# Bias tiles turned by PE transposes, the memory source in the bias buffer's free part, and output projections begun inside the attentions' last steps

## The chip, the cores and the metric

The kernel runs on one NeuronCore of a Trainium2 chip. The metric is the device time of one execution in microseconds. TensorE is called PE here, VectorE DVE, ScalarE ACT, GpSimd POOL and SyncE SP, as in the profile.

## The reference, cut to what matters

Three transformer blocks follow each other on one sequence of 256 tokens with 1024 features, all in float32. The first has a gated linear attention and "moba", a causal attention with a bias by relative position; the second a stick-breaking attention, a memory attention and 32 routed experts; the third two layers, l0 and l1, each a feed-forward (ffn1), a mixer, a memory attention and a feed-forward again. The change lies in moba and in the mixers and memory attentions of the two layers. What these compute:

```python
# moba (8 heads), dsa (8 heads, over selected keys), band (16 heads); masked keys get -inf
logits = einsum('bqhd,bshd->bhqs', q, k) * dh ** -0.5 + bias_table[bucket(qpos - kpos)]
o = einsum('bhqs,bshd->bqhd', softmax(logits), v)
# diff (4 heads, two maps each, one bias per head)
attn = p[:, :, 0] - lam * p[:, :, 1]
out_b = rmsnorm(einsum('bhqs,bshe->bqhe', attn, v), subln_g) * (1.0 - lambda_init)
# l0: h + concat([dsa, diff]) @ w_out; l1: h + band @ w_out
# memory attention of each layer, m = rmsnorm(mem, src_gain)
k, v = split(m @ wkv, 2); k = rmsnorm(k); q = rmsnorm(h @ wq)
o = softmax(q @ k.T * M_DIM ** -0.5) @ v;  h = h + o @ wo
```

## The kernel before

Activations lie feature-major in SBUF as tiles of 128 features x 256 tokens: `tile(X, i)`, T = 256, P = 128, eight tiles for 1024 features. Weights come as a stream of 2 MB chunks through five slots `W`; SP's queue loads a chunk when the semaphore `released` says that the one five before it is done with, and PE raises `released` in order, on the first matmul behind a chunk's last use (`end_chunk`, `pending`). Every engine's program is one straight list, so the order of work is the order of the code; engines wait for each other by semaphores. PSUM has eight banks of 128 x 512: banks 0 to 3 are a ring that `ring_bank` deals out in turn, 4 to 7 are given by name (`banks.begin`). A bank that is begun again is waited for until the engine that reads it has emptied it.

All of PE's matmuls but a few go through the helper `mm` and so show as L600. One float32 matmul leaves two records in the trace. `turn_probs` (L890) transposes with one record each.

A biased attention runs in `softmax_pairs`: step p issues the scores of heads 2p and 2p+1 into two ring banks, then whatever `fill(p)` holds, then the values of pair p-3 (bank 7), then the transposes of the probabilities of pair p-2 (banks 5 and 6). DVE takes the maxima and scales the exponentials, ACT makes the exponentials (L1728) and copies turned probabilities and outputs out of PSUM (L1647). The exponentials of a head wait until the probabilities of four heads before are turned, and ACT copies turned probabilities after a step's exponentials.

The bias of a head is added by PE: a table in DRAM is read with overlapping rows into `A`, 512 columns a head, so that a matmul with the anti-identity `REV` as stationary operand puts the reversed bias into the bank, and the scores are accumulated on top. `load_bias` fetches this on POOL's queue.

In the layers the memory keys and values (`layer_memory_half`, eight halves of eight or four matmuls each) are the fill of diff and of band; their source is loaded into `H` when the projections are done with it, and ACT multiplies it by its gains (`memory_gains`). Behind the attention stands `down(f"{l}_w_out", ...)`, the output projection, in banks 4 to 7 with the sums of the memory keys' norm between its parts, and then `memory`: two query units, the scores of four heads, transposes, results, projection. `gates` of the first block are the fill of moba.

The norms outside `BY_LOG` take a square root on ACT and a reciprocal on DVE; those in it take a logarithm and an exponential on ACT.

## Time and profile before

| | us |
|---|---|
| median of 3 runs | 3049.65 (3047.19 to 3058.12) |
| profiled execution | 3052.73 |
| its span | 3050.9 |
| PE busy | 2906.7 |
| DVE busy | 1356.4 |
| ACT busy | 600.1 |
| first bias to gates 7's end, moba | 157.2 to 231.4 |
| diff and dsa with the output projection, l0 | 2034.0 to 2137.2 |
| band with the output projection, l1 | 2689.7 to 2790.7 |

A busy PE is one with a matmul in flight; matmuls overlap, so a row's duration is longer than the distance to the next start. A row of the timeline merges instructions of one kind; in brackets stands how long the engine was idle before it and what released it.

### The profile page before, as it was taken

How to read it: one execution, taken by the hardware profiler on the slowest of the kernel's cores; microseconds unless marked ns; L12 is line 12 of the kernel's file. 1: busy time of each engine (PE TensorE's matmuls, PEld its weight loads, DVE VectorE, ACT ScalarE, POOL GpSimd, SP SyncE). 2: the span in 40 equal slices, each digit the busy share in tenths (PEclk: the TensorE clock that was granted, in tenths of full speed). 3: DMA queues.
4: the chain of work that ended last, by engine and by line, in shares of the span. 5: the costliest groups of instructions: out<-in, count | busy, mean ns of one | idle time of the engine just before them, and what ended most of it. 6: DMA issues, size and time to landing. Idle time of an engine off the chain costs nothing.

```text
span 3050.9 us, 44763 instructions
## 1 busy us (share of the span) xinstructions
PE 2906.7 (95%) x18718; PEld 2251.9 (74%) x18718; DVE 1356.4 (44%) x2555; ACT 600.1 (20%) x1249; POOL 13.0 (0%) x22
## 2 busy tenths in 40 slices
PE   8999999999999898999899899999999999989999
PEld 7988999868543333343343699986899999967999
DVE  5432896422211111112111576655566665643665
ACT  2220331221211111111011210233210110242210
POOL 0000000000000000000000000000000000000000
PEclk9999999999899999999999999999999999999999
DMA  6333544334899999999999644541344444523341
GB/s 247 139 111 140 192 166 169 136 110 166 352 432 431 432 432 430 433 431 433 429 431 432 277 174 173 193 165 60 111 170 169 187 166 174 213 97 111 139 166 70
DMA packets 39026, 723.83 MB, mean 237 GB/s; under 512 B 4220, under 2 KB 4348, under 8 KB 7504
## 3 DMA queue, kind: packets, MB, share of 16 engines
q1 hardware_dynamic: 35280, 705.73, 57.7%
q0 software_dynamic: 3584, 15.74, 1.5%
q8 instruction: 127, 2.08, 0.3%
q14 instruction: 35, 0.29, 0.0%
HBM read 720.32 MB, written 1.12 MB: 236 GB/s over the span
## 4 chain that ended last, share of the span: by engine, by line
PE 83%; DMA 12%; DVE 2%; ACT 2%; issue 1%; SPq 0%; POOL 0%; ACTq 0%; DVEq 0%
PE ps L600 64%; DMA sb_weights<-stream 12%; PE ps L1462 9%; PE ps L1482 4%; PE ps L1440 2%; PE ps L1400 2%; PE ps L890 1%; DVE sb_x L2436 0%; ACT sb_weights L1647 0%; PE ps L1428 0%; DVE sb_h L2187 0%; ACT sb_weights L1728 0%; DVE sb_squares L2155 0%; PE ps L1495 0%; ACT sb_k L2041 0%
## 5 line engine op out<-in xcount | busy, mean ns | idle before, releaser
L600 PE MATMUL ps<-sb_h,sb_weights 128*128 128x128 f32 (+1 forms) x3488 | 565.1, 317 | 23.5 <-DMA sb_weights<-stream 7.9
L600 PEld LDWEIGHTS ps<-sb_h,sb_weights 128*128 128x128 f32 x3488 | 503.8, 193 | 66.4 <-issue 12.9
L1462 PE MATMUL ps<-sb_weights,sb_k 128*64 128x512 f32 x1536 | 340.2, 595 | 16.5 <-DMA sb_weights<-stream 9.8
L2834 DVE TENSOR_TENSOR sb_v<-ps,sb_small 128x256 f32<-128x256 f32 x128 | 48.4, 420 | 667.1 <-PE ps L1428 667.1
L600 PE MATMUL ps<-sb_weights 128*128 128x256 f32 (+1 forms) x1744 | 302.9, 331 | 8.0 <-ACT sb_weights L1647 6.5
L600 PEld LDWEIGHTS ps<-sb_weights 128*128 128x128 f32 x1744 | 269.2, 192 | 35.4 <-ACT sb_weights L1647 7.1
L1462 PEld LDWEIGHTS ps<-sb_weights,sb_k 128*64 128x64 f32 x1536 | 109.6, 137 | 216.5 <-issue 204.1
L600 PE MATMUL ps<-sb_v,sb_weights 128*128 128x128 f32 x2240 | 265.4, 276 | 0.0
L600 PEld LDWEIGHTS ps<-sb_v,sb_weights 128*128 128x128 f32 x2240 | 257.6, 192 | 0.0
L600 PE MATMUL ps<-sb_a,sb_weights 128*128 128x128 f32 (+1 forms) x1512 | 205.5, 293 | 1.1 <-DVE sb_a L2614 1.1
L1482 PE MATMUL ps<-sb_weights,sb_k 128*64 128x512 f32 x768 | 173.5, 605 | 31.2 <-DMA sb_weights<-stream 30.7
L600 PEld LDWEIGHTS ps<-sb_a,sb_weights 128*128 128x128 f32 x1512 | 192.9, 192 | 8.2 <-issue 1.5
L1482 PEld LDWEIGHTS ps<-sb_weights,sb_k 128*64 128x64 f32 x768 | 55.5, 139 | 133.6 <-issue 133.6
L600 PE MATMUL ps<-sb_r,sb_weights 128*128 128x128 f32 x1256 | 149.8, 276 | 0.0
L600 PEld LDWEIGHTS ps<-sb_r,sb_weights 128*128 128x128 f32 x1256 | 144.9, 192 | 0.0
L2041 ACT ACTIVATE sb_q<-ps 128x512 f32<-128x512 f32 x64 | 38.2, 597 | 461.2 <-PE ps L1462 461.2
L1462 PE MATMUL ps<-sb_a,sb_k 128*64 128x512 f32 x512 | 113.4, 595 | 7.9 <-ACT sb_k L2041 7.9
L1792 ACT ACTIVATE sb_v<-ps 128x256 f32<-128x256 f32 x120 | 46.0, 384 | 341.1 <-PE ps L600 334.3
L1647 ACT ACTIVATE sb_v<-ps 128x256 f32<-128x256 f32 (+1 forms) x59 | 24.6, 416 | 367.6 <-PE ps L600 367.6
L2480 DVE TENSOR_TENSOR sb_weights<-ps,sb_v 128x256 f32<-128x256 f32 x160 | 63.2, 420 | 74.2 <-PE ps L600 73.9
L2331 DVE TENSOR_TENSOR sb_weights<-sb_weights 128x1024 f32<-128x1024 f32 (+1 forms) x80 | 94.8, 1186 | 0.0
L1462 PEld LDWEIGHTS ps<-sb_a,sb_k 128*64 128x64 f32 x512 | 38.8, 137 | 71.3 <-issue 71.3
(358 smaller groups left out, 3403.1 us busy)
## 6 DMA issues: line engine op xcount, KB each, us to landing
sb_weights<-stream SPq DMA_DIRECT2D x72, 4096.0 KB, 28.1
sb_weights<-stream SPq DMA_DIRECT2D x142, 2048.0 KB, 7.8
sb_a<-stream SPq DMA_DIRECT2D x24, 4096.0 KB, 27.7
sb_a<-tables POOLq DMA_DIRECT2D x2, 2048.0 KB, 16.6
sb_a<-tables POOLq DMA_DIRECT2D x2, 1536.0 KB, 14.1
sb_weights<-stream SPq DMA_DIRECT2D x2, 1024.0 KB, 7.6
sb_a<-tables POOLq DMA_DIRECT2D x2, 1024.0 KB, 7.8
sb_h<-mem POOLq DMA_DIRECT2D x2, 1024.0 KB, 5.1
```

Source lines behind the costliest of these rows:

```text
L600: ins = pe.matmul(out, lhsT, rhs, start=start, stop=stop, skip_group_check=skip)
L890: ins = pe.transpose(PS[b][:, n * P:(n + 1) * P], probs[:, t * T + s * P:t * T + (s + 1) * P], ident)
L1400: ins = pe.matmul(PS[4 + m // 2][:, (m % 2) * T:(m % 2 + 1) * T], Y_TOK[:, m * P:(m + 1) * P], SPREAD, start=False, stop=last, skip_group_ ...
L1440: ins = pe.matmul(ps[:, q * PAIR:(q + 1) * PAIR], H_TOK[:, t * D + d * P:t * D + (d + 1) * P], PICK[:, t * PAIR:(t + 1) * PAIR], start=t = ...
L1462: ins = pe.matmul(ps[own[e], :], XG[:, k * PAIR + e * LOT:k * PAIR + (e + 1) * LOT], w[e](k * 512, 512), start=k == 0, stop=k == KT - 1)
L1482: ins = pe.matmul(ps[n][own[e], :], HID[:, k * PAIR + e * LOT:k * PAIR + (e + 1) * LOT], w[e]((k % 4) * D + n * 512, 512), start=k == 0, s ...
L1647: act.activation(dst, src(b), func, scale=scale).then_inc(banks.emptied[b], 1)
L1792: act.activation(KEPT[i], PS[b][:, 0:T], ACT.Copy).then_inc(sem("kept"), 1)
L2041: act.activation(dst, PS[fill[0]][:, 0:cols], ACT.Copy).then_inc(L.emptied[fill[0]], 1)
L2331: dve.tensor_tensor(part(0, 1), part(1, 1), part(0, 1), ALU.subtract).then_inc(done, 1)
L2480: return dve.tensor_tensor(by_tile(dst)[:, :, t * P:(t + 1) * P], by_tile(PS[b][:, 0:T]), by_tile(kept), ALU.add)
L2834: ins = dve.tensor_tensor(by_lot(z, s), by_lot(PS[TURNED[c][0]][:, :], s), bias.unsqueeze(3).broadcast_to([P, 2, 2, LOT]), ALU.add)
```

## The change

The bias of a head is now 256 columns of `A` and one transfer, with the table stored the other way round. Three 128 x 128 transposes, each with a block of the table as stationary operand and `REV` as moving one, put it into the bank (`biases`); the scores are accumulated on top as before. The masked corner is one memset. The half of `A` that this frees takes the memory source (`MEM`), which POOL fetches right behind the bias, and ACT scales in two parts during the projections.

Fills move. In band, halves 0 to 6 of the memory units fill steps 0 to 6 (before: 0 to 7 in steps 2 to 9), with units in banks 7 and 4 in place of the ring; in diff, seven halves remain. Half 7 goes into the memory attention, between scores 2 and 3, with its weight chunk kept back (`keep_back`, `end_kept`) and scores 3 in bank 5. moba's gates go to bank 4. The output projections (`layer_out`) use banks 0 to 3; their first 40 matmuls stand in the attentions' last three steps, before values and transposes; the sums of the memory keys and the rest come after. For l0 the diff tiles come first, and w_out's two chunks are swapped in the stream. The sums of `l0_nsub` go behind dsa's first pair. Three norms join `BY_LOG`. Band starts when the first two key tiles are normalized (`band_ready`).

```diff
+            def biases(b, head):
+                for s, t in ((0, 0), (0, 1), (1, 1)):
+                    at = head * T + (t - s) * P
+                    pe.matmul(PS[b][:, t * T + s * P:t * T + (s + 1) * P], A[:, at:at + P], REV[:, :],
+                              start=s == t == 0, stop=False, is_transpose=True, skip_group_check=True)
...
-            def softmax_pairs(name, fill=lambda p: None):
+            def softmax_pairs(name, fill=lambda p: None, ready=lambda p: None):
...
                         for e in range(2):
-                            for t in range(2):
-                                cols = keys(True, t)
-                                mm(PS[bs[e]][:, cols], REV[:, :], A[:, (2 * p + e) * 512:(2 * p + e + 1) * 512][:, cols],
-                                   t == 0, False, True)
-                                if a.get("mask") is not None:
-                                    mm(PS[bs[e]][:, cols], ident, a["mask"][:, cols], False, False, True)
+                            biases(bs[e], 2 * p + e)
+                            for t in range(2 if a.get("mask") is not None else 0):
+                                mm(PS[bs[e]][:, keys(True, t)], ident, a["mask"][:, keys(True, t)], False, False, True)
...
+        OUT_IN_TAIL = [(range(4), range(4)), (range(4), range(4, KT)), ((4,),)]
...
+            def layer_out(l, js, ms=range(KT)):
+                name, src = f"{l}_w_out", tiles(O, 8) if l == "l1" else tiles(O, 4, 4) + tiles(O, 4)
+                if js[0] == 0:
+                    for i in range(ms[0] // 2, ms[-1] // 2 + 1):
+                        banks.begin(pe, (name, i), i)
+                if js[0] in (0, 4) and ms[0] == 0:
+                    out_weights[0] = next_chunk()
+                w, last = out_weights[0], js[-1] == KT - 1
+                order = [(j, 2 * i + m) for i in range(4) for j in js for m in range(2)] if last else [
+                    (j, m) for j in js for m in ms]
+                for j, m in order:
+                    if m == ms[0] and l == "l0":
+                        if j >= 4:
+                            banks.wait_emptied(pe, ("dsa", "out", j - 4))
+                        elif j % 2 == 0:
+                            norm_part(pe, "l0_nsub", j // 2)
+                    elif m == ms[0]:
+                        banks.wait_emptied(pe, ("band", "out", j))
+                    ins = mm(PS[m // 2][:, (m % 2) * T:(m % 2 + 1) * T], w[:, (j % 4) * D + m * P:(j % 4) * D + (m + 1) * P],
+                             src[j], j == 0 and m % 2 == 0, j == KT - 1, True)
...
                     logits(2)
-                    logits(3)
+                    layer_memory_half(l, 7)
+                    logits(3, bank=5)
...
-            softmax_pairs("moba", lambda p: fm_unit("gates", h, p))
-            fm_unit("gates", h, 7)
+            softmax_pairs("moba", lambda p: fm_unit("gates", h, p, bank=4))
+            fm_unit("gates", h, 7, bank=4)
...
+                        for n in {0: (0, 1), 1: (2,), 5: ()}.get(i, (i + 2,)):
+                            layer_memory_half(l, n, bank=4 if n == 6 else None)
...
-                    sums("l0_nsub")
                     pe.wait_ge(sem("dsa_mask"), 2)
-                    softmax_pairs("dsa")
-                    banks.wait_emptied(pe, ("dsa", "out", 3))
+                    def dsa_fill(p):
+                        if p == 0:
+                            sums("l0_nsub", (5, 6))
+                        if p >= 4:
+                            layer_out(l, *OUT_IN_TAIL[p - 4])
+                    softmax_pairs("dsa", dsa_fill)
...
-                    softmax_pairs("band", lambda p: layer_memory_half(l, p - 2) if 2 <= p <= 9 else None)
-                    banks.wait_emptied(pe, ("band", "out", 7))
-                down(f"{l}_w_out", tiles(O, 8), {1: lambda: pe.wait_ge(sem("subln_scaled"), 1)} if l == "l0" else {},
-                     between={1: lambda: sums(f"{l}_nmk")})
+                    def band_ready(p):
+                        if p % 2 == 0 and p < 8:
+                            norm_part(pe, "l1_nk", p // 2)
+                        if p == 3:
+                            for c in range(2):
+                                banks.wait_emptied(pe, ("l1_v", "common", c))
+                    def band_fill(p):
+                        if p < 7:
+                            layer_memory_half(l, p, bank=7 if p < 2 else 4)
+                        elif p > 7:
+                            layer_out(l, *OUT_IN_TAIL[p - 8])
+                    softmax_pairs("band", band_fill, band_ready)
+                sums(f"{l}_nmk", (5, 6))
+                layer_out(l, (5,))
+                layer_out(l, (6, 7))
...
-                    squares("l0_nsub", lambda eng, part: [banks.wait_emptied(eng, ("diff", "out", 2 * part + q)) for q in range(2)])
-                    softmax_pairs("dsa")
+                    squares_only("l0_nsub", lambda eng, part: [banks.wait_emptied(eng, ("diff", "out", 2 * part + q)) for q in range(2)])
+                    softmax_pairs("dsa", lambda p: roots("l0_nsub") if p == 0 else
+                                  squares_only("l0_nmk", x_ready("l0_mem_k")) if p == 4 else None)
...
-                for key in [("iq", 0), ("iq", 1)] if l == "l0" else [("l1_v", "common", 1)]:
-                    banks.wait_filled(pool, key)
-                pool.dma_start(H[:, :], mem3_d).then_inc(sem(f"{l}_mem_loaded"), 16)
+                pool.dma_start(MEM[l], mem3_d).then_inc(sem(f"{l}_mem_loaded"), 16)
```

In PE's list, band begins as follows before the change: the projection's last rows, then bias (moving `sb_a`, stationary `sb_reversal`) and scores (`sb_k,sb_q`) of pair 0, and the bias of pair 1 at once.

```order
1019 L600 MATMUL ps<-sb_weights,sb_r 128x256 x8
1020 L600 MATMUL ps<-sb_a,sb_reversal 128x128
1021 L600 MATMUL ps<-sb_a,sb_reversal 128x256
1022 L600 MATMUL ps<-sb_a,sb_reversal 128x128
1023 L600 MATMUL ps<-sb_a,sb_reversal 128x256
1024 L600 MATMUL ps<-sb_k,sb_q 128x128 x2
1025 L600 MATMUL ps<-sb_k,sb_q 128x256 x2
1026 L600 MATMUL ps<-sb_a,sb_reversal 128x128
```

The same place after the change, where `sb_a,sb_weights` is half of a memory unit:

```order
990 L603 MATMUL ps<-sb_weights,sb_r 128x256 x8
991 L885 MATMUL ps<-sb_reversal,sb_a 128x128 x6
992 L603 MATMUL ps<-sb_k,sb_q 128x128 x2
993 L603 MATMUL ps<-sb_k,sb_q 128x256 x2
994 L603 MATMUL ps<-sb_a,sb_weights 128x256 x8
995 L885 MATMUL ps<-sb_reversal,sb_a 128x128 x6
```

Four bias matmuls of a pair became six transposes, and a memory half moved between the first pairs.

In PE's list, dsa ends as follows before the change: values (`sb_weights,sb_v`), transposes of probabilities (`sb_const,...`, L890), and behind the last values the output projection (`sb_weights 128x256`) with the sums of the memory keys.

```order
770 L890 MATMUL ps<-sb_const,sb_squares 128x128 x6
771 L600 MATMUL ps<-sb_weights,sb_v 64x256 x2
772 L600 MATMUL ps<-sb_weights,sb_v 64x128 x2
773 L890 MATMUL ps<-sb_const,sb_weights 128x128 x6
774 L600 MATMUL ps<-sb_weights,sb_v 64x256 x2
775 L600 MATMUL ps<-sb_weights,sb_v 64x128 x2
776 L890 MATMUL ps<-sb_const,sb_squares 128x128 x6
777 L600 MATMUL ps<-sb_weights,sb_v 64x256 x2
778 L600 MATMUL ps<-sb_weights,sb_v 64x128 x2
779 L600 MATMUL ps<-sb_weights 128x256 x16
780 L600 MATMUL ps<-sb_squares,sb_const 128x256 x4
```

The same place after the change (L934 is `turn_probs` there):

```order
737 L934 MATMUL ps<-sb_const,sb_squares 128x128 x6
738 L603 MATMUL ps<-sb_weights 128x256 x16
739 L603 MATMUL ps<-sb_weights,sb_v 64x256 x2
740 L603 MATMUL ps<-sb_weights,sb_v 64x128 x2
741 L934 MATMUL ps<-sb_const,sb_weights 128x128 x6
742 L603 MATMUL ps<-sb_weights 128x256 x16
743 L603 MATMUL ps<-sb_weights,sb_v 64x256 x2
744 L603 MATMUL ps<-sb_weights,sb_v 64x128 x2
745 L934 MATMUL ps<-sb_const,sb_squares 128x128 x6
746 L603 MATMUL ps<-sb_weights 128x256 x8
747 L603 MATMUL ps<-sb_weights,sb_v 64x256 x2
748 L603 MATMUL ps<-sb_weights,sb_v 64x128 x2
```

Between the last three groups of values and transposes, 16, 16 and 8 matmuls of the projection now stand.

On ACT, the start of dsa before the change has the roots of `l0_nsub` (Sqrt, `sb_squares<-ps`) ahead of the first exponentials (`sb_softmax_stats` rows), with a table load on either side.

```order
414 L1699 ACTIVATE sb_squares<-ps,sb_const 128x512 x2
415 L1728 ACT_TABLE_LOAD
416 L1728 ACTIVATE sb_weights,sb_softmax_stats<-ps,sb_softmax_stats 128x128
417 L1728 ACTIVATE sb_weights,sb_softmax_stats<-ps,sb_softmax_stats 128x256
418 L1728 ACTIVATE sb_weights,sb_softmax_stats<-ps,sb_softmax_stats 128x128
```

After the change:

```order
415 L1788 ACTIVATE sb_weights,sb_softmax_stats<-ps,sb_softmax_stats 128x256
416 L1745 ACT_TABLE_LOAD
417 L1762 ACTIVATE sb_squares<-ps,sb_const 128x512
418 L1763 ACTIVATE sb_squares<-sb_squares 128x512
419 L1762 ACTIVATE sb_squares<-ps,sb_const 128x512
420 L1763 ACTIVATE sb_squares<-sb_squares 128x512
421 L1788 ACTIVATE sb_squares,sb_softmax_stats<-ps,sb_softmax_stats 128x128
```

The roots, now logarithms and exponentials, stand between the exponentials of pair 0 and those of pair 1.

## Rows read from the trace of the kernel before

**Rows 1.** The page, part 1: busy time, share of the span, instructions.

```profile
PE 2906.7 (95%) x18718; PEld 2251.9 (74%) x18718; DVE 1356.4 (44%) x2555; ACT 600.1 (20%) x1249; POOL 13.0 (0%) x22
```

**Rows 2.** The page, part 4: the chain that ended last.

```profile
PE 83%; DMA 12%; DVE 2%; ACT 2%; issue 1%; SPq 0%; POOL 0%; ACTq 0%; DVEq 0%
```

**Rows 3.** PE's timeline, steady part of band: start us, us, instructions merged.

```profile
2715.17 0.87 PE L600 MATMUL ps<-sb_weights,sb_v 128*64 128x256 f32 x8
2715.97 0.87 PE L890 MATMUL ps<-sb_const,sb_squares 128*128 128x128 f32 x6
2716.68 1.48 PE L600 MATMUL ps<-sb_a,sb_reversal 128*128 128x128 f32 x8
2718.09 0.93 PE L600 MATMUL ps<-sb_k,sb_q 64*128 64x128 f32 x8
2718.95 3.72 PE L600 MATMUL ps<-sb_h,sb_weights 128*128 128x256 f32 x16
2722.60 0.87 PE L600 MATMUL ps<-sb_weights,sb_v 128*64 128x256 f32 x8
```

**Rows 4.** Line L890 in band: count, duration ns min/median/max, first and last start.

```profile
L890 PE MATMUL ps<-sb_const,sb_weights x24: 272/273/330, 2707.5 to 2753.4; 128*128 128x128 f32 x24
```

**Rows 5.** PE's timeline from the last projection before band to the query.

```profile
2686.22 3.62 PE L600 MATMUL ps<-sb_weights,sb_r 128*128 128x256 f32 x16
2693.49 2.90 PE L600 MATMUL ps<-sb_a,sb_reversal 128*128 128x128 f32 x8 [3.65 <-issue]
...
2761.24 7.14 PE L600 MATMUL ps<-sb_weights 128*128 128x256 f32 x32 [0.68 <-ACT sb_weights L1647]
...
2790.67 7.07 PE L600 MATMUL ps<-sb_h,sb_weights 128*128 128x256 f32 x32
```

**Rows 6.** Waits of PE, 2689 to 2791: us in total, times, longest.

```profile
PE ps L600 <- ACT sb_weights L1728: 2.9, 4, 0.8
PE ps L600 <- ACT sb_weights L1647: 1.6, 2, 1.0
```

**Rows 7.** PE's timeline, diff and dsa of l0 up to the query.

```profile
2034.02 1.58 PE L600 MATMUL ps<-sb_a,sb_reversal 128*128 128x128 f32 x8
...
2076.30 1.97 PE L600 MATMUL ps<-sb_squares,sb_const 128*128 128x256 f32 x8 [1.08 <-ACT sb_squares L1681]
2078.10 0.38 PE L600 MATMUL ps<-sb_a,sb_reversal 128*128 128x128 f32 x2
...
2081.67 0.49 PE L600 MATMUL ps<-sb_a,sb_reversal 128*128 128x128 f32 x2
...
2097.56 0.87 PE L600 MATMUL ps<-sb_weights,sb_v 128*64 128x256 f32 x8 [2.58 <-ACT sb_weights L1647]
...
2137.21 7.07 PE L600 MATMUL ps<-sb_h,sb_weights 128*128 128x256 f32 x32
```

**Rows 8.** Two stretches: length, PE, PEld, DVE, ACT, POOL busy, granted clock, DMA share.

```profile
2100.00:2108.00 8.00, 6.26 (x26) 4.13 (x27) 6.56 (x7) 3.71 (x8) 0.00 (x0) 0.50 0.01 2
2710.00:2750.00 40.00, 38.34 (x215) 25.63 (x214) 15.60 (x65) 13.20 (x54) 0.00 (x0) 1.00 0.15 53
```

**Rows 9.** DVE's timeline: the first maxima of dsa, behind the mask.

```profile
2081.77 0.62 DVE L2305 TENSOR_REDUCE sb_softmax_stats<-ps 128x1 f32<-128x128 f32 x2 [11.02 <-PE ps L600]
```

**Rows 10.** PE's timeline in moba: pairs 1 and 3.

```profile
168.35 1.55 PE L600 MATMUL ps<-sb_a,sb_reversal 128*128 128x128 f32 x8 [1.75 <-ACT sb_weights L1728]
...
188.61 1.55 PE L600 MATMUL ps<-sb_a,sb_reversal 128*128 128x128 f32 x8 [0.83 <-ACT sb_weights L1728]
```

**Rows 11.** DVE's timeline in moba: the copy of gate 0.

```profile
167.90 0.68 DVE L2253 TENSOR_TENSOR sb_a<-ps,sb_rstd 128x512 f32<-128x512 f32 x1
```

**Rows 12.** PE's timeline, memory attention of l0: scores 3, and the next query.

```profile
2158.39 2.08 PE L600 MATMUL ps<-sb_r,sb_q 128*128 128x256 f32 x4 [1.90 <-ACT sb_weights L1728]
...
2183.71 7.07 PE L600 MATMUL ps<-sb_h,sb_weights 128*128 128x256 f32 x32
```

**Rows 13.** DMA issues, 2000 to 2250: count, KB each, median us to landing.

```profile
sb_weights<-stream SPq DMA_DIRECT2D x14, 2048.0 KB, 7.8
```

More of the change, by code:

```diff
@@ L186, in stream_of @@
             out += [columns(w)]
-        out += [columns(g("mem_wkv")), rows(g("w_out")), columns(g("mem_wq")), rows(g("mem_wo"))]
+        w = rows(g("w_out"))
+        out += [columns(g("mem_wkv")), w[::-1] if l == "l0" else w, columns(g("mem_wq")), rows(g("mem_wo"))]
         out += [up_pairs(g("ffn2_wg"), g("ffn2_wu")), rows_22(g("ffn2_wd"))]
@@ L651, in fm, with fm_unit @@
                             between[2 * c + u]()
-            def fm_unit(name, src, u, norm=None):
+            def fm_unit(name, src, u, norm=None, bank=None):
                 w = next_chunk() if u % 2 == 0 else half_used[0]
                 half_used[0] = w
-                b = ring_bank((name, u))
+                b = ring_bank((name, u)) if bank is None else banks.begin(pe, (name, u), bank)
                 for m in range(2):
@@ L693, in layer_memory_half @@
                 if not second:
-                    half_used[0] = next_chunk() if u % 2 == 0 else half_used[0]
-                    ring_bank(key)
-                w, (b, _) = half_used[0], banks.of[key]
+                    memory_used[0] = next_chunk() if u % 2 == 0 else memory_used[0]
+                    ring_bank(key) if bank is None else banks.begin(pe, key, bank)
+                w, (b, _) = memory_used[0], banks.of[key]
                 for j in range(KT):
@@ L753, in down @@
                     end_chunk()
+            out_weights = [None]
+            def layer_out(l, js, ms=range(KT)):
[18 more added lines that the diff above has]
+                             src[j], j == 0 and m % 2 == 0, j == KT - 1, True)
+                    if last and j == KT - 1 and m % 2:
+                        ins.then_inc(banks.filled[m // 2], 1)
+                if js[-1] % 4 == 3 and ms[-1] == KT - 1:
+                    end_chunk()
             def begin_norm(name):
@@ L795, in first_sums, with sums @@
                 ins.then_inc(banks.filled[b], 1)
-            def sums(name):
+            def sums(name, at=None):
                 n = NORMS[name]
@@ L802, in sums @@
                 for u in range(-(-groups // 2)):
-                    b = ring_bank((name, u))
+                    b = ring_bank((name, u)) if at is None else banks.begin(pe, (name, u), at[u])
                     for g in range(2 * u, min(2 * u + 2, groups)):
@@ L818, in softmax @@
                         b = ring_bank((name, "logits", i))
-                        biased = a["bias"] is not None
-                        causal = "causal" in a
-                        for t in range(2 if biased else 0):
-                            cols = keys(causal, t)
-                            mm(PS[b][:, cols], REV[:, :], A[:, i * 512:(i + 1) * 512][:, cols], t == 0, False, True)
-                            if a.get("mask") is not None:
-                                mm(PS[b][:, cols], ident, a["mask"][:, cols], False, False, True)
                         for t in range(2):
                             qs, ks = a["q"](i, t), a["k"](i)
-                            cols = keys(causal, t)
+                            cols = keys("causal" in a, t)
                             for j in range(len(qs)):
-                                ins = mm(PS[b][:, cols], qs[j], ks[j][:, 0:cols.stop - cols.start], not biased and j == 0,
+                                ins = mm(PS[b][:, cols], qs[j], ks[j][:, 0:cols.stop - cols.start], j == 0,
                                          j == len(qs) - 1, True)
@@ L1074, in query, with logits @@
                     fm_unit(f"{name}_q", tiles(H, 8), u, qn if u == 0 else None)
-                def logits(h):
-                    b = ring_bank((name, "logits", h))
+                def logits(h, bank=None):
+                    b = ring_bank((name, "logits", h)) if bank is None else banks.begin(pe, (name, "logits", h), bank)
                     banks.wait_emptied(pe, (f"{name}_q", h // per_unit))
@@ L1887, in project_kept, with memory_gains @@
                 keep(3, fourth, banks.emptied[fourth])
-            def memory_gains(l):
+            def memory_gains(l, part):
                 act.wait_ge(sem(f"{l}_mem_loaded"), 16)
-                for i in range(KT):
-                    act.activation(tile(H, i), tile(H, i), ACT.Identity, scale=S(f"{l}_mem_src_norm", i, i + 1)
+                for i in range(4 * part, 4 * part + 4):
+                    act.activation(tile(MEM[l], i), tile(MEM[l], i), ACT.Identity, scale=S(f"{l}_mem_src_norm", i, i + 1)
                                    ).then_inc(sem(f"{l}_mem_scaled"), 1)
```

106 lines of the change are left out of this document (56 added, 50 removed).

## The prediction

> **What bounds the kernel now.** I read the page's busy times first: TensorE (PE) is busy 95% of the span, the vector engine (DVE) 44%, the scalar engine (ACT) 20% [rows 1]. The chain that ended last is 83% PE and 12% DMA, the latter the experts' weights, which the change leaves alone [rows 2]. So outside the experts a microsecond of PE work removed, or of PE waiting filled, comes off the span unless something else ends later. Touched are four attentions (moba; diff and dsa in layer l0; band in layer l1) and, in each layer, the output projection and the memory attention behind them. There I read PE's timeline in starts: the distance of two starts prices what lies between, without the overlap of pipelined ends. A stage's span less the sum of its parts is what it loses.
>
> **Term 1, the bias.** In the steady part of band a pair of heads takes 1.41 us for its bias (2716.68 to 2718.09, eight records for four matmuls), 0.86 for scores, 3.65 for half a memory unit, 0.80 for values, and 0.71 for six transposes of probabilities (2715.97 to 2716.68), so 0.118 each [rows 3]. The change does a pair's bias with six transposes of that 128x128 shape, each with a stationary operand of its own, as those have. Before: 20 pairs (moba 4, diff 4, dsa 4, band 8) x 1.41 = 28.2; after: 20 x 0.71 = 14.2. That is -14.0, all of it PE time, and it is contained in terms 2 to 4. The dsa masks stay ordinary matmuls. The records of such a transpose last 0.273 though they start 0.118 apart [rows 4]; I take the starts, since only they delay the next instruction.
> The Trainium skill ("TensorE: Matmul & The Clock Gate", Part 4: PE-mode transpose) gives some 275 ns for a transpose inside a kernel. The record's length agrees, the spacing does not; by the page's figure 120 transposes would be an estimated 33.0 us, and this term a loss of 4.8.
>
> **Term 2, band (l1).** From the end of the projection (2686.22 + 3.5) to the first query behind the output projection (2790.67) it is 101.0 us [rows 5]. The work in it, by starts: 8 pairs x (1.41 + 0.86) = 18.2, eight memory halves x 3.6 = 28.8, values 6.4, transposes 5.7, output projection with the key sums (from 2761.24) 29.4; together 88.5. So 12.5 is waiting or a low clock: the first bias waits 3.65 and then takes 2.90 instead of 1.48 [rows 3, 5]; four waits on the exponentials of L1728 (2.9) come from the ring of four banks, which scores share with memory halves; two on ACT's copies (1.6) are the bare tail [rows 6].
> After, the ring holds scores alone, memory halves use banks 7 and 4, and the opening waits only for the first two key tiles. Halves fill the first steps too, 40 of the projection's 64 matmuls stand in the tail's three steps, and the key sums and one more tile cover the last output's copy. Work is 88.5 - 5.6 (bias) - 3.6 (the last half, moved on) = 79.3. The eighth step has no fill: its values wait for the copies of an earlier pair's turned probabilities, which ACT makes only after a pair's exponentials. I take 1.0, as the longest such wait in band is now, bounds 0 and 2.6 (the longest in dsa) [rows 6, 7]. Result 80.3, **-20.7**.
>
> **Term 3, diff and dsa (l0).** From the first bias (2034.02) to the query at 2137.21 it is 103.2 [rows 7]. Work: diff runs without a gap to 2075.1, 41.1; sums 1.8; dsa 4 pairs x 3.6 (2078.10 to 2081.67) = 14.5; its values and transposes 4 x 1.51 = 6.0; projection and sums 29.4; together 92.8. Lost: 10.4, of which 2.58 at 2097.56, and from 2100 to 2108 the granted clock is 0.50, that is 1.2 GHz, after a stretch in which PE mostly waited [rows 7, 8].
> After, work is 92.8 - 5.6 - 3.5 = 83.7. The sums of l0_nsub stand behind the first pair, so nothing waits for their squares. On ACT a table load and four root steps now stand ahead of pair 1's exponentials; behind them queue those, the copies of turned probabilities and, on PE, the fourth pair's banks. The fourth step has no fill, so its values feel that: I take 1.8 (0 to 2.6), and 0.4 for diff's last probabilities, which lose a half's cover. The mask is no new wait: DVE is done with it at 2070.75 and idles 11.0 [rows 9]; PE will ask some 9 us earlier than 2078.1, and DVE, whose gaps in diff are PE's lateness, ends up to 2 earlier. The margin is thin; 0 to 1, I take 0. Result 85.9, **-17.3**. The reciprocals that leave DVE for a logarithm and an exponential on ACT cost nothing, since projection tiles cover them; uncovered they are four steps of that size at about 0.68 [rows 11], 2.8.
>
> **Term 4, moba.** Bias -2.8. Two ring waits stand here, 1.75 and 0.83 [rows 10]. The gates get bank 4 for themselves, so gate 1 needs gate 0 copied, which DVE does late, at 167.90 + 0.68 [rows 11]. PE, which came to the ring at 166.6, comes there at 167.5 (0.7 less, bias and scores of pair 1 more) and waits 1.2. Of the 2.6 in waits 1.4 is saved. New: branch_a opens bank 4 and waits for the copy of gate 7, 0.68 and its signals, 0.9; the whole projection queues behind. -2.8 - 1.4 + 0.9 = **-3.3**.
>
> **Term 5, memory attention.** The half moved into each layer's memory attention, 3.5, lands where scores 3 wait 1.90 for a bank [rows 12]; they get bank 5. The chain of exponentials, copies and first result goes on under the half, later only by one more copy on ACT (0.68 for that size on DVE, [rows 11]). PE comes to its first projection about as now: +0.2 per layer, bounds -1 and +3.5. **+0.4**.
>
> **What costs nothing, and its cover.** The gain multiplications go to ACT during the projections; uncovered they are eight of half the size of the copy at 0.68 [rows 11], some 3 in each layer. The bias transfer is halved and the memory source is fetched right behind it on POOL's queue, a stage ahead of use. A weight chunk kept until the memory attention holds back four releases and SP's queue with them; the next block's first chunk is then issued near 2160, lands in 7.8 and is needed at 2183.71 [rows 12, 13]. The projection's last four banks now end half as far apart, but the memory projection already ends so and its query at 2183.71 follows without a wait.
>
> **Sum.** -20.7 - 17.3 - 3.3 + 0.4 = -40.9. The profiled run took 3052.73, 3.1 above the median of the runs: 3052.7 - 40.9 = 3011.8, and on the median's scale 3009. All bounds against it make -30, all for it -46. The forecast's own range is 3003 to 3019.
>
> **Rivals.** (a) *The waits only move.* The softmax chain, not the order, sets the pace; only the bias is gained, 3049.7 - 14 = 3036. For it: the exponentials stand before most of today's waits. Against: in band's steady part ACT is busy 13.2 of 40 us and DVE 15.6 [rows 8], and probabilities are asked for two steps after their scores. 0.08.
> (b) *Transposes run 0.273 apart*, their record's length: 120 x 0.155 = 18.6 more, 3028. Against: six of them start within 0.71 [rows 3]. 0.06. The page named in term 1 is the case for it.
> (c) *Weights late.* If the four chunks released together landed 32 us after (four times 7.8), the next block would stand some 8 in each layer: 3009 + 16 = 3025. Against: the first alone is needed at once, and DMA is 0.15 busy here [rows 8]. 0.06.
> (d) *Slower: the clock.* If PE falls to 1.2 GHz in the attentions because twelve instead of six transposes stand in a pair's step, each microsecond of work costs a second one. Ahead of their projections the attentions hold about 165 us after the change: 3009 + 165 = 3174; 41 us at the low clock eat the gain, 56 make it slower by 0.5%. For it: 8 us at 0.50 in dsa. Against: that followed waits, which shrink, and 40 us of band stand at 1.00 with a transpose train in every step [rows 8]. 0.04. The same page says that the full clock does not engage for transposes; the row just named does not bear that out.
>
> **Numbers.** Forecast 0.76. A difference under 0.5% (15 us) can hardly be told from no change here. Faster: the forecast, (b) and (c), 0.88; same: (a), 0.08; slower: (d), 0.04. The range, 3002 to 3030, takes in the forecast, (b) and (c).
>
> **What would show it.** Right: 120 bias transposes 0.12 apart, or a little more at a train's ends; in band no waits but one near 1, and about 80 us from projection to query; in dsa one near 2 and the clock at 1.00; none at scores 3; about 1 before branch_a. Wrong: bias transposes that start over 0.2 apart, a clock of 0.50 in a pair's step, a wait for weights in the second feed-forward block, or values that wait in every step.

## The result, and the profile after

The changed kernel takes 3009.85 us in the median of 4 runs (3008.61 to 3013.56); the kernel before, in runs beside it, 3052.59 (3047.19 to 3058.12). The ratio is 0.9867 with a 95% interval of 0.9854 to 0.9881: about 1.3% faster, as forecast (3009, range 3002 to 3030). Three of the four runs of before are those of the table above, whose median was 3049.65. The profiled execution took 3009.02, its span 3007.2.

The page's part 1 of the kernel after (busy time, share, instructions) answers to [rows 1]: PE's busy time falls by 20 us, the span by 44, so more than half of what went was time in which PE stood idle.

```profile
PE 2887.1 (96%) x18678; PEld 2233.1 (74%) x18678; DVE 1332.3 (44%) x2547; ACT 604.8 (20%) x1256; POOL 9.9 (0%) x19
```

PE's timeline of the kernel after (start us, us, instructions merged, idle time before them and what ended it): two waits of moba, then l0 from its first bias to the query behind its memory attention, then band from the last projection to its query. It answers to [rows 3, 5, 7, 10, 12].

```profile
168.44 7.17 PE L603 MATMUL ps<-sb_h,sb_weights 128*128 128x256 f32 x32 [1.18 <-DVE sb_a L2317]
...
227.83 22.47 PE L603 MATMUL ps<-sb_weights 128*128 128x256 f32 x103 [0.83 <-issue]
...
2026.44 0.88 PE L885 MATMUL ps<-sb_reversal,sb_a 128*128 128x128 f32 x6
...
2060.30 0.52 PE L934 MATMUL ps<-sb_const,sb_squares 128*128 128x128 f32 x3 [0.40 <-DVE sb_squares L3062]
...
2061.95 0.92 PE L603 MATMUL ps<-sb_weights,sb_v 128*128 128x256 f32 x4 [0.47 <-ACT sb_weights L1707]
...
2078.30 0.87 PE L603 MATMUL ps<-sb_weights,sb_v 128*64 128x256 f32 x8 [1.26 <-ACT sb_weights L1707]
...
2113.39 7.07 PE L603 MATMUL ps<-sb_h,sb_weights 128*128 128x256 f32 x32
...
2159.58 7.07 PE L603 MATMUL ps<-sb_h,sb_weights 128*128 128x256 f32 x32
...
2661.49 3.62 PE L603 MATMUL ps<-sb_weights,sb_r 128*128 128x256 f32 x16
2664.97 0.85 PE L885 MATMUL ps<-sb_reversal,sb_a 128*128 128x128 f32 x6
...
2687.91 0.82 PE L885 MATMUL ps<-sb_reversal,sb_a 128*128 128x128 f32 x6
2688.66 0.93 PE L603 MATMUL ps<-sb_k,sb_q 64*128 64x128 f32 x8
...
2703.69 3.70 PE L603 MATMUL ps<-sb_weights,sb_a 128*128 128x512 f32 x8 [0.61 <-ACT sb_v L1703]
...
2711.57 0.87 PE L603 MATMUL ps<-sb_weights,sb_v 128*64 128x256 f32 x8 [1.07 <-ACT sb_weights L1707]
...
2746.66 7.07 PE L603 MATMUL ps<-sb_h,sb_weights 128*128 128x256 f32 x32
```

Read the starts. In band the first bias follows the projection at once, where 3.65 us stood. A pair's bias takes 0.75 (2687.91 to 2688.66), where it took 1.41. Two waits are left, 0.61 and 1.07. From the projection's end (2661.49 + 3.5) to the query it is 81.7, before 101.0. In l0 three waits are left, 2.13 together, where the prediction counts 10.4 as lost.

In stretches (length, busy time of PE, PEld, DVE, ACT and POOL, granted clock, DMA share) the kernel after reads as follows for diff with dsa, band, and 8 us of the memory attention; the second and third answer to [rows 8].

```profile
2026.44:2113.39 86.95, 84.83 (x463) 65.55 (x461) 49.91 (x184) 36.37 (x106) 0.00 (x0) 1.00 0.11 43
2664.97:2746.66 81.69, 80.01 (x449) 60.34 (x449) 32.35 (x120) 32.35 (x105) 0.00 (x0) 1.00 0.14 52
2136.00:2144.00 8.00, 6.50 (x34) 5.22 (x33) 3.26 (x14) 4.12 (x12) 0.00 (x0) 1.00 0.79 295
```

The clock column is 1.00 in all three. Put together, from start to start:

| stage | before | after | difference | predicted |
|---|---|---|---|---|
| moba, to the projection behind it | 74.24 | 70.86 | -3.4 | -3.3 |
| diff and dsa, to the query | 103.19 | 86.95 | -16.2 | -17.3 |
| memory attention, l0 | 46.50 | 46.19 | -0.3 | +0.2 |
| band, to the query | 100.95 | 81.67 | -19.3 | -20.7 |
| memory attention, l1 | 45.65 | 46.19 | +0.5 | +0.2 |
| sum | | | -38.7 | -40.9 |

The other 5.0 us of the span's 43.7 lie in stretches where the change leaves PE's work as it was, 4.0 of them between moba and l0 (1802.61 and 1798.61).

### The profile page after: what moved, and what is told of

Same layout as the page of the kernel before. It is cut to its first block, busy times and chain, and to the rows that moved or that the text cites. A ratio compares the mean times of both kernels' runs of the same rounds, so it can differ in the third digit from the quotient of the medians.

```text
span 3007.2 us, 44681 instructions
## 1 busy us (share of the span) xinstructions
PE 2887.1 (96%) x18678; PEld 2233.1 (74%) x18678; DVE 1332.3 (44%) x2547; ACT 604.8 (20%) x1256; POOL 9.9 (0%) x19
## 4 chain that ended last, share of the span: by engine, by line
PE 83%; DMA 11%; DVE 3%; ACT 2%; issue 1%; SPq 0%; POOL 0%; ACTq 0%; DVEq 0%
PE ps L603 63%; DMA sb_weights<-stream 11%; PE ps L1506 9%; PE ps L1526 5%; PE ps L1444 2%; PE ps L1484 2%; PE ps L934 1%; DVE sb_x L2500 0%; ACT sb_weights L1707 0%; PE ps L1472 0%; PE ps L885 0%; DVE sb_h L2251 0%; DVE sb_softmax_stats L2369 0%; ACT sb_squares L1788 0%; DVE sb_squares L2219 0%
## 5 line engine op out<-in xcount | busy, mean ns | idle before, releaser
L603 PE MATMUL ps<-sb_h,sb_weights 128*128 128x128 f32 (+1 forms) x3360 | 533.2, 313 | 22.7 <-DMA sb_weights<-stream 8.5
L603 PEld LDWEIGHTS ps<-sb_h,sb_weights 128*128 128x128 f32 x3360 | 477.8, 192 | 60.5 <-DVE sb_h L2251 11.6
L603 PE MATMUL ps<-sb_a,sb_weights 128*128 128x128 f32 (+1 forms) x1640 | 234.9, 300 | 1.1 <-DVE sb_a L2680 1.1
L603 PEld LDWEIGHTS ps<-sb_a,sb_weights 128*128 128x128 f32 x1640 | 216.5, 191 | 13.2 <-issue 3.5
```

The source lines that it names most:

```text
L603: ins = pe.matmul(out, lhsT, rhs, start=start, stop=stop, skip_group_check=skip)
```

## The experiments

Theory: PE pays for a bias transpose the distance of starts; the waits came from an order in which the softmax chain was asked too early, so work put in between removes them. Rivals: the waits only move; transposes cost their record's length; transposes hold the clock down. The times of the kernel before beside the runs were 3051.83 for the first four, 3054.15 (one run) for the next four, 3052.65 for the last three. Since one trace gives the stages to some 0.1 us and whole runs differ by several us, stages decide.

### The turned bias alone

On the kernel before, `biases` in place of the four matmuls, the tables turned, nothing else.

> The kernel before with the turned bias alone: tables stored the other way round, one transfer, three transposes a head; every order, bank and norm as it was. Theory (PE work): a pair's bias falls from 1.41 to 0.75 us, 20 pairs, 13.2 us less work; behind the bias today's waits for exponentials and copies grow a little, so some 9 to 13 come off the whole, about 3041 on the scale of 3052, and the rest of the change is worth some 30. Rival (the waits take it back): in moba, band and dsa the waits for exponentials grow by what the bias gives up, and under 5 come off. Rival (everything is the turn): over 25.

3034.23 us, ratio 0.9946 (0.9930 to 0.9963). PE's waits in moba and at band's opening, of this run:

```profile
168.09 0.85 PE L846 MATMUL ps<-sb_reversal,sb_a 128*128 128x128 f32 x6 [2.40 <-ACT sb_weights L1729]
...
2682.01 0.85 PE L846 MATMUL ps<-sb_reversal,sb_a 128*128 128x128 f32 x6 [1.16 <-ACT sb_weights L1729]
```

The waits take back a part: 1.75 became 2.40 [rows 10], and band's first wait for exponentials, 0.46 before, became 1.16. A wait that [rows 6] does not show, 1.52 ahead of band's first memory half, became 2.23. PE's and ACT's rows at that place in the kernel before:

```profile
2704.01 3.69 PE L600 MATMUL ps<-sb_h,sb_weights 128*128 128x256 f32 x16 [1.52 <-issue]
```

```profile
2699.82 3.30 ACT L1893 ACTIVATE sb_h<-sb_h,sb_small 128x256 f32<-128x256 f32 x8
```

ACT's row is the gain multiplications of the memory source. They stood between the exponentials of pair 0 and those of pair 1, and PE went on just behind the first exponentials that follow them. The change moves them into the projections; no run undoes that alone.

Moba fell by 2.1 and band by 3.9 (97.3, in the second trace of before, to 93.4 from its first bias), where the work fell by 2.6 and 5.3. The median fell by 17.6, outside the expected 9 to 13; by the interval of the ratio it is 11 to 21, so a fall by the work alone (13.2) is not excluded. From here to the changed kernel it is 24.3 by stages and 24.4 in the medians, where I expected some 30.

### The output projection's first part out of the tail

```diff
-                        if p >= 4:
-                            layer_out(l, *OUT_IN_TAIL[p - 4])
...
+                for part in OUT_IN_TAIL:
+                    layer_out(l, *part)
                 sums(f"{l}_nmk", (5, 6))
```

(In band the same two lines for p > 7 go as well.)

> The changed kernel with the output projections whole behind the attentions: their first 40 matmuls no longer stand in the last three steps. Theory (those matmuls cover the softmax chain's last steps): the bare steps wait for exponentials and copies again, 3 to 5 us in band (81.7 becomes about 85.5), 4 to 8 in dsa (86.9 becomes about 93, with a stretch at the lower clock as before the change), whole about 3020. Rival (probabilities are asked for two steps late anyway, cover or no cover): each stage within 1 us of the changed kernel, 3010 to 3012.

3022.63 us. PE's waits in dsa of this run; band's last three steps show the same 2.57, 0.97 and 0.97.

```profile
2085.98 0.87 PE L603 MATMUL ps<-sb_weights,sb_v 128*64 128x256 f32 x8 [2.57 <-ACT sb_weights L1705]
2088.63 0.87 PE L603 MATMUL ps<-sb_weights,sb_v 128*64 128x256 f32 x8 [0.97 <-ACT sb_weights L1705]
2091.28 0.87 PE L603 MATMUL ps<-sb_weights,sb_v 128*64 128x256 f32 x8 [0.97 <-ACT sb_weights L1705]
```

Dsa with diff became 91.67 and band 86.39, 4.7 more each, and the new waits sum to 4.5. The tail's cover is worth 9.4 us in the two layers. The low clock that I expected in dsa did not come (1.00 in 2086:2094, around these waits).

### Each bias transposed twice

```diff
-                for s, t in ((0, 0), (0, 1), (1, 1)):
+                for s, t in 2 * ((0, 0), (0, 1), (1, 1)):
```

> The changed kernel with each head's three bias transposes issued twice, the second set starting the bank anew; the result is the same. 120 more transposes. Theory (PE pays by the distance of starts, 0.12 us): 14 us of work more, less up to 2 that today's waits absorb; 3022 to 3024, the granted clock in the attentions at 1.00. Rival (0.273 each, the record's length): 33 more, 3043. Rival (transposes hold the clock down): stretches at 0.50 in the steps of band and dsa, some 20 us more than the theory's time for each 20 us of work done in them.

3022.30 us. A stretch of its PE timeline, and the window of band:

```profile
2679.57 1.47 PE L885 MATMUL ps<-sb_reversal,sb_a 128*128 128x128 f32 x12
2680.97 0.93 PE L603 MATMUL ps<-sb_k,sb_q 64*128 64x128 f32 x8
```

```profile
2673.72:2759.33 85.61, 85.20 (x498) 65.56 (x498) 32.26 (x120) 32.31 (x105) 0.00 (x0) 1.00 0.14 50
```

Twelve transposes take 1.40 from start to start, 0.117 each. The stages grew by 1.4, 3.3 and 3.9 while waits of 1.2, 1.7 and 1.3 vanished under the new work: 12.8 for 120 transposes, 0.107 each. The granted clock is 1.00 with 96 of them in band's eight steps. Both rivals that speak of transposes fall. That the whole came out at the expected 3022 to 3024 is in part chance: the stages grew by 8.6 and not by 12, and 4.5 more lie in the untouched stretch between moba and l0 (1803.1 after 1798.6).

### The last memory half back in the attention

```diff
-                    layer_memory_half(l, 7)
                     logits(3, bank=5)
...
-                        if p < 7:
+                        if p < 8:
                             layer_memory_half(l, p, bank=7 if p < 2 else 4)
```

(In diff `5: ()` becomes `5: (7,)`.)

> The changed kernel with the last memory half back in the attention (band's step without fill, diff's last step) and nothing between scores 2 and 3 of the memory attention, scores 3 still in bank 5. Theory (in the memory attention the half lies under the chain of exponentials and copies): the two memory attentions stay near 46 us, between 44 and 46.5, with waits of 2 to 4 us or a low clock in place of the half; band grows by 2.5 (3.6 less the wait of 1.07), diff by 3; whole 3013 to 3016. Rival (the half is plain PE work wherever it stands): the memory attentions fall by 3.5 each, to 42.7, band and diff grow by 2.5 and 3, whole 3008 to 3009.

3023.91 us (3016.78 to 3025.32; the profiled one is the lowest). Diff with dsa grew by 2.7 and band by 2.5, as expected. The memory attentions, with 3.4 us less work in each, did not stay: they grew from 46.19 to 47.72 and 48.21. PE's timeline right behind scores 2 and 3 (four transposes each, then the first result), and the window to compare with the last one above:

```profile
2137.21 0.66 PE L934 MATMUL ps<-sb_const,sb_weights 128*128 128x128 f32 x4 [1.98 <-DVE sb_weights L2345]
2138.80 1.08 PE L934 MATMUL ps<-sb_const,sb_weights 128*128 128x128 f32 x4 [0.93 <-DVE sb_weights L2345]
2140.37 2.05 PE L603 MATMUL ps<-sb_weights,sb_v 128*128 128x256 f32 x4 [0.49 <-ACT sb_weights L1706]
```

```profile
2136.00:2144.00 8.00, 4.90 (x15) 3.24 (x16) 4.60 (x18) 5.54 (x18) 0.00 (x0) 0.60 0.16 67
```

Without the half PE waits 3.4 us, then works at a granted clock of 0.60, mostly its lower level of 1.2 GHz: four transposes take 0.66 and 1.08, against 1.04 for eight with the half. The half is better than free there: it costs less than nothing by 1.5 and 2.0 us. In l0 the 3.4 us of work that went were replaced by 5.0: the waits grew by 2.4 in sum, and the other 2.6 are the lower clock, so by this sum the half would cost 1.0 if the clock stayed up in both. The memory attentions missed the expected 44 to 46.5, and the whole the expected 3013 to 3016. The stages make 8.7 of the 14.1 us; the other three executions lie 6 to 9 above the profiled one, and no trace shows where.

### Band opened late

Band waits for all of its keys and values before the first bias (`norm_done(pe, "l1_nk")` at p = 0, in place of a part per two pairs).

> The changed kernel with band waiting at its opening for all of the normalized keys and values, as before the change, in place of the first two key tiles. Theory (the early start fills a wait that nothing else fills): PE stands 3.5 us ahead of the first bias again, perhaps 1.4 more for a low clock behind it; from the end of the projection to the query band takes 85.2 to 86.6 in place of 81.7. Rival (what is late at the opening comes back later, since the chain of the first pairs ends no sooner): the stage stays within 1 us of 81.7 because the waits of 0.61 and 1.07 behind it go.

3020.16 us, one run. PE's timeline at the opening, and the window behind it:

```profile
2673.21 1.51 PE L885 MATMUL ps<-sb_reversal,sb_a 128*128 128x128 f32 x6 [3.80 <-DVE sb_v L2431]
2674.65 1.65 PE L603 MATMUL ps<-sb_k,sb_q 64*128 64x128 f32 x8
...
2681.32 0.82 PE L885 MATMUL ps<-sb_reversal,sb_a 128*128 128x128 f32 x6
```

```profile
2673.00:2681.00 8.00, 7.79 (x29) 6.04 (x30) 1.48 (x6) 1.72 (x8) 0.00 (x0) 0.60 0.56 197
```

From the projection's end to the query it is 88.5, 6.8 more: 3.9 of waiting, and 2.9 of the lower clock that follows it (six transposes 1.44 from start to start, twice the 0.75; then 0.82 again). The later waits of 0.61 and 1.06 stay, so the rival falls; the stage is 2 us above the expected 85.2 to 86.6, because the lower clock cost twice what I put on it. By the row, what ended the wait were values (`sb_v`), which the changed kernel asks for only at the fourth step. The wait and its clock together are the largest gain in band that a run has undone by itself.

### Gates 1 and 7 in other banks

```diff
-            softmax_pairs("moba", lambda p: fm_unit("gates", h, p, bank=4))
-            fm_unit("gates", h, 7, bank=4)
+            softmax_pairs("moba", lambda p: fm_unit("gates", h, p, bank=7 if p == 1 else 4))
+            fm_unit("gates", h, 7, bank=0)
```

> The changed kernel with gate 1 in bank 7 and gate 7 in bank 0, the other gates in bank 4 as they are. Theory (both waits of moba are waits for bank 4): the 1.18 before gate 1 and the 0.83 before the projection behind gate 7 go, and moba to the projection's start falls from 70.9 to 68.9. Rival (the softmax chain sets the pace): a wait for exponentials before a later bias takes the place of the first, and moba ends within 0.5 of 70.9 less the 0.83.

3007.86 us, one run; moba 68.57, 2.3 less, and no wait left in it. Both of its waits were for bank 4.

### ACT's copies ahead of its exponentials

In ACT's `softmax_pairs` the copies of turned probabilities stand before the step's exponentials, and band's first memory values before both.

> The changed kernel with ACT copying a step's turned probabilities ahead of the step's exponentials, not behind them, and in band the first copy of memory values ahead of both. Theory (the values of a step without fill wait for the copies only because ACT makes four exponentials first): the waits of 0.61 and 1.07 in band and of 1.26 in dsa go, band 81.7 to 80.1, dsa with diff 86.9 to 85.7, nothing else moves, 3 us in all. Rival (the exponentials, 1.2 us later, are then what the next transposes or biases wait for): the same waits come back one step on and the stages stay within 0.5.

3014.28 us, one run, with the longest stretch between moba and l0 of all traces, 1805.1. By stages: dsa with diff 85.64 (the 1.26 is gone), band 81.0 (the 0.61 is gone, the 1.07 is not), 2.0 in place of the expected 3. ACT's and then PE's timeline around band's step without fill:

```profile
2714.03 0.87 ACT L1707 ACTIVATE sb_weights<-ps 128x384 f32<-128x384 f32 x2 [3.99 <-PE ps L934]
...
2716.37 0.41 ACT L1707 ACTIVATE sb_weights<-ps 128x256 f32<-128x256 f32 x1
```

```profile
2716.84 0.87 PE L603 MATMUL ps<-sb_weights,sb_v 128*64 128x256 f32 x8 [1.07 <-ACT sb_weights L1707]
```

The turned probabilities (384 columns) are copied by 2714.9, and PE still waits, until the copy of an output (256 columns) at 2716.37 has ended. So in band it looks to be bank 7, where the values go, that was still full; the run that moves this copy (both moves together, below) bears it out. In dsa the step without fill is the first with values, and no output is in that bank.

### The kernel before, a second time

> The kernel before, unchanged, for a second trace. If the low granted clock in the fourth step of dsa (0.50 over 8 us), in both memory attentions and behind band's opening belongs to the kernel's own waits, it stands there again, and dsa with diff takes 103, the memory attentions 45.6 to 46.5. If it comes and goes between executions, dsa with diff takes 99 to 100 and the stretch between moba and l0, which the change leaves alone, is some 4 us shorter or longer than the 1802.6 of the first trace.

3047.09 us. The waits in dsa's last steps are those of the first trace, 2.57, 0.97, 0.97 and 0.68, yet the clock is not; the window of those steps against the 0.50 in [rows 8]:

```profile
2094.00:2102.00 8.00, 4.40 (x37) 2.94 (x38) 7.93 (x9) 3.60 (x10) 0.00 (x0) 1.00 0.00 0
```

Diff with dsa took 99.81, 3.4 less than in the first trace. The memory attention kept its low clock (0.66 in 2150:2160, the stage 46.55), band's opening its wait of 3.65. The untouched stretch between moba and l0 took 1800.6; over all thirteen traces it runs from 1798.2 to 1805.1, without order by kernel. One difference can be seen: the same twenty records behind a wait for `sb_h` took 6.27 us in the first trace of before and 4.58 in that of after. So the dip in dsa comes and goes between executions of the same kernel. How often it comes two traces can't say; the median of before, 3052 to 3053, lies nearer to the first trace than to this one. Against this trace the turned bias alone (its span 3031.0 against 3045.3) gives 4.5 in diff and dsa (99.81 to 95.27) and 10.5 in its three stages, within the expected 9 to 13; 2.4 more lie in the untouched stretch. The second trace is 4.7 below the median that the 17.6 was taken from, and what that median holds beyond the trace no row shows.

### Both moves together, and the memory attention's order

The first kernel has the gates' banks and, on ACT, the copy of the output, then the turned probabilities, then the exponentials. The second adds on PE:

```diff
                     result(0)
+                    turned(2)
                     onward([0])
-                    turned(2)
                     result(1)
+                    turned(3)
                     onward([1])
-                    turned(3)
```

and lets `onward` wait for the fourth output only at the matmul that reads it.

> The changed kernel with gates 1 and 7 in banks 7 and 0, and with ACT making a step's copies (the output of the pair behind, then the turned probabilities) ahead of the step's exponentials, band's first copy of memory values first of all. Theory (band's wait of 1.07 stayed in the run before because PE's bank 7, not the turned probabilities, was still uncopied): it goes now, band 81.7 to 80.0, diff and dsa 86.9 to 85.6, moba 70.9 to 68.6, 5.3 us in all, about 3004.5. Rival (the wait of 1.07 has a third cause): band stays at 81.0, 4.3 in all. A difference of 4 to 5 us is about what the untouched stretches differ between executions, so the stages decide.

> The same with the memory attention's order changed on PE alone: transposes of heads 2 and 3 ahead of the projection parts that wait for an output's copy, and the last part waiting for the fourth output only behind its first two matmuls. Theory (PE waits there for one copy at a time, and 0.44 us of transposes or 0.88 of matmuls fit in): the waits of 0.66, 0.47 and 0.56 shrink to under 0.3 each, each memory attention from 46.2 to about 44.9, whole about 3002. Rival (ACT is what ends late, so the wait only moves to the next copy): the memory attentions stay within 0.4 of 46.2.

The first: 3006.57 us, ratio to before 0.9850 (0.9835 to 0.9866); moba 68.57, dsa with diff 85.63, band 79.87 from its first bias (81.69), no wait left in it, so the rival of a third cause falls: 5.4 by stages. The second: 3001.95 us (3001.32 to 3004.53), ratio 0.9838 (0.9825 to 0.9852); each memory attention 44.29, 1.9 less. Its PE timeline there:

```profile
2138.34 3.72 PE L603 MATMUL ps<-sb_weights 128*128 128x256 f32 x16 [0.22 <-ACT sb_weights L1709]
```

The 0.66 is 0.22, the 0.47 and the 0.56 are gone. This version beats both kernels, by 9.2 us of stages against the changed one and by 7.9 in the medians.

### The three norms back at square root and reciprocal

`l0_nsub`, `l0_nmk` and `l1_nmk` leave `BY_LOG` again; all else as in the changed kernel.

> The changed kernel with the three norms that it added to the logarithms back at a square root on ACT and a reciprocal on DVE. Theory (only where ACT and DVE have the projection's cover is it free): band and both memory attentions within 0.3 of the changed kernel; dsa longer by 1 to 3 us, since two reciprocals on DVE, at an estimated 0.7 each, stand ahead of the maxima of pair 2 and a second table load of 1.28 ahead of pair 1's exponentials, and the wait of 1.26 in the fourth step grows by what they add. Rival (all of it is hidden): dsa with diff 86.9 as it is.

3025.02 us. DVE's, then PE's timeline in dsa:

```profile
2076.47 3.35 DVE L2219 RECIPROCAL sb_squares<-sb_squares 128x512 f32<-128x512 f32 x1
...
2080.65 3.35 DVE L2219 RECIPROCAL sb_squares<-sb_squares 128x512 f32<-128x512 f32 x1
```

```profile
2088.31 1.55 PE L603 MATMUL ps<-sb_weights,sb_v 128*64 128x256 f32 x8 [8.01 <-ACT sb_weights L1707]
```

A reciprocal of 512 columns takes 3.35 us, not the 0.7 that I put on it, and two of them stand ahead of the maxima of pair 2. PE's wait of 1.26 becomes 8.01, 6.75 more for two reciprocals of 3.35, with a lower clock behind it (0.87 becomes 1.55); dsa with diff takes 95.65, 8.7 more. Each memory attention takes 48.09, 1.9 more, since the residual sums queue on DVE behind two more. Band is as it was. Expected were 1 to 3 in dsa and nothing else.

## Why the prediction was right, point by point

**The total** was right within a microsecond, more closely than its parts, and that closeness is luck. The stages gave 38.7 of the predicted 40.9, and the untouched stretches, which vary by several us between executions, gave the rest in this pair of runs. Against the second trace of before the stages give 35.6. The base moved too: with the fourth run the median of before is 3052.59, not 3049.65, so the medians differ by 42.7. What is right is the account by stages.

**Term 1** (14.0): right in kind, 0.8 too large. A pair's bias takes 0.75, not 0.71, so 13.2. That PE pays the distance of starts and not the 0.273 of the record is shown by the doubled transposes.

**Term 2** (20.7; measured 19.3): the opening, the ring and the tail went as said. The opening is worth 6.8 when it alone is undone, the tail 4.7, the bias 5.3 of work; that the waits for exponentials came from a ring shared with memory halves was not tried by itself (they are gone after). The term names no cause for the 1.52 ahead of the first memory half. The prediction books the moved gain multiplications only as costing nothing; with them in the projections that wait is gone too. The residual was put at 1.0 and is 1.68: 1.07 at the step named, and 0.61 at a place not foreseen, where half 6 needs bank 4 and ACT has the copy of the first memory values behind a pair's exponentials. Another 0.3 is the longer bias. And one reason was wrong. "Its values wait for the copies of an earlier pair's turned probabilities" holds in dsa; in band it was the copy of an output out of bank 7. Both stand behind the exponentials on ACT, so the size came out by luck.

**Term 3** (17.3; measured 16.2): the residual of 2.2 is 2.13, but by luck: the fourth step waits 1.26 and not 1.8, diff's last probabilities and values 0.87 and not 0.4. The 1.1 that is missing lies in the work, 0.3 of it the longer bias; the rest is not resolved. Two things were mis-read. The low clock "after a stretch in which PE mostly waited" was counted as the kernel's own; it is 3.4 us that stand in one of two executions, and against the other the term gives 12.9. And the sentence on the reciprocals prices only the four steps that take their place on ACT, at 2.8; for `l0_nsub` these take 2.5 in the trace after (2069.61 to 2072.11), ahead of pair 1's exponentials, where no projection tile covers them. The reciprocals themselves got no price there, and 0.7 from me later, though the kernel before has the operation at 3.35. With two of them dsa takes 8.7 us more. So putting the sums of `l0_nsub` behind the first pair pays here only with the logarithms. The term survived because the logarithms were in the change, not because the step was priced well.

**Term 4** (3.3; measured 3.4): both waits at their places and sizes, 1.18 (1.2) and 0.83 (0.9). That both are bank 4's is shown by moving the two gates.

**Term 5** (+0.4; measured +0.2, as -0.3 and +0.5): the size is right, but the account left out the clock. In l0 of the kernel before the stretch behind scores 3's wait ran partly at the lower clock:

```profile
2156.00:2166.00 10.00, 7.63 (x26) 5.46 (x25) 5.88 (x24) 7.18 (x20) 0.00 (x0) 0.66 0.33 143
```

The half takes 3.44 where PE stood 2.06 between scores 2 and 3, 1.4 more, and from scores 3 to the first projection it is now 4.50 in place of 6.18, 1.7 less, at a clock of 1.00. "About as now" came out because these two cancel. Without the half the memory attention is longer, not equal, because PE waits and then runs at 1.2 GHz.

**Rivals.** (a) holds for a part of the turned bias alone, 2.7 of 13.2, and for moba's waits: of 2.58, 2.01 came back, at bank 4. (b) and (d) are refuted by the doubled transposes. The Trainium skill ("TensorE: Matmul & The Clock Gate", Part 4: PE-mode transpose) gives some 275 ns for a bf16 one in a kernel, and no full clock for them. The records here, in float32, agree with that length (272 to 332 ns), but PE pays the 0.117 us between starts, at a granted clock of 1.00. (c): PE comes to the query at 2159.58 without a wait, and to that of l1 at 2792.85.

## What to carry to other kernels

Price an operation from a row of that operation: a reciprocal of 512 columns took 3.35 us, five times the copy of the same size, and two of them on DVE cost dsa 8.7. Where PE waits for long, look for a low clock behind the wait as well, and put independent work there: the memory half, moved there, cost less than nothing. A wait put down to an engine's copies names neither the copy nor the bank: look which copy ended just before the wait did, then put the copies that free a bank ahead of the work that nobody awaits yet.

## What the runs showed of the hardware

With transposes issued as matmuls with their own stationary block the granted clock stayed at 1.00 here, among other matmuls (96 bias transposes in 86 us, twelve together). A wait of 3.80 us at band's opening was followed at once by the lower of the two clocks (0.60 over 8 us, six transposes in twice the time), as was one of 3.65 in both traces of before (the first bias in 2.90, not 1.48); one of 3.65 in the turned bias alone was followed by it only behind two more waits, some 8 us on. Waits of 2.57, 0.97 and 0.97 in a row were followed by it in the first trace of before, not in the second, nor in that of the turned bias alone, nor in dsa or band of the bare tail. A wait of 8.01 was followed by it at once (0.75 over 8 us). One kernel's executions lie 1 to 12 us apart; in the traces the stretch between moba and l0, in which no edit touched PE's work, differs by up to 6.9. An edit worth 2 us can be read from a stage of one trace, but hardly from medians of four runs.
